# Differential attention: scaling and difference of the two softmax maps made in the turn, by two accumulated products with diagonal matrices

## The chip, the cores and the metric

The kernel is one program on one core of a Trainium2 chip. The metric is device time in microseconds (us) of a whole execution. Three runs of the kernel before took 2820.64, 2817.66 and 2817.2 us, median 2817.66.

Engines are named as in the profile: PE is TensorE's matmul, PEld its weight load, DVE is VectorE, ACT ScalarE, POOL GpSimd and SP SyncE, which issues most DMAs.

## What is computed

The reference is one layer of a hybrid decoder for a prompt of 1024 tokens and eight sample sequences of one new token each, with 2048 tokens in a paged cache. Everything is float32. The part that the change touches is the attention of the prompt:

```
def diff_attn_core(q, k, v, q_pos, k_pos, lam):
    s = einsum("bqhd,bkhd->bhqk", q, k) * (DA_QK ** -0.5)
    s = where(k_pos[None, :] <= q_pos[:, None], s, -inf)
    p = softmax(s, axis=-1).reshape(b, DA_HEADS, 2, tq, tk)
    w = p[:, :, 0] - lam * p[:, :, 1]
    return einsum("bhqk,bkhd->bqhd", w, v)
```

There are 4 heads, each with two maps of 64 columns for query and key and one value of 128 columns. The two feed-forward blocks, the projections and a recurrent branch (RWKV-7) in chunks of 128 tokens stand before and after it in the same program.

## The kernel before

All engines run one program each, whose order is written out by hand; they meet at semaphores. The stages follow each other: feed-forward 1, the projection of query, key and value, the projection for the recurrent branch and the gates, the attention, the recurrent branch in eight chunks, the merge, the output projection, feed-forward 2. The dense stages split each float32 operand in a high and a low part and make three products of each tile (L1792).

The attention has 32 steps, one for each block of 128 queries and each head: `qi = step // 4` is the block of queries, `h = step % 4` the head. A step looks at `n = (qi + 1) * 128` keys, so its width grows from one block of 128 keys to eight, and the 32 steps have 4 * (1 + ... + 8) = 144 blocks. The tile `probs` (`pr` in the code) has two slots, `s = step % 2`, of two maps each. In one step:

- PE makes the scores of a later step in PSUM (L2021), two steps ahead while `qi < 4` and one step ahead after that.
- DVE adds the causal mask to the last block (L1493), takes the maximum of each row (L1495) and scales it (L1496), for each map.
- ACT takes the exponential of each map from PSUM to `probs`, with the row's sum as a by-product (L1062). These are probabilities without their division by the sum.
- DVE takes the reciprocals of the two sums (L1512), multiplies the second by lambda (L1513), scales the second map by it (L1515), and then makes `p1 * inv1 - p2` over the first map (L1517). It tells PE by `w_ready`.
- PE turns each block of the first map to have keys on the partitions (L2042), into PSUM banks 4 and 5. It tells ACT by `w_trans_lo` for the first four blocks and `w_trans_hi` for the others.
- ACT copies the turned blocks to `w_trans` (`wT`, L1086) and tells PE by `w_moved`.
- PE sums the squares of the step before (L2027) and multiplies the values with `w_trans`, block by block (L2056). ACT copies the result (L1095) and squares it (L1100).

Woven in is the attention of the samples. Their softmax is made on DVE in three pieces behind steps 0 to 2 (L1454 to L1474). Their values are 32 groups of four pages, one megabyte a group, which SP loads to a ring of two slots (L560, `value_ring`) and PE weights (L1998) at the places that `FILL_STEP` names: one group in most steps from step 4 on, two in steps 17, 19, 22, 25, 26 and 28. A group is loaded once the second group before it has been used. The four pages are four DMAs.

The tile `tmp` (`T`) has two rows of 1032 columns. Before the attention it holds the gates, whose DMAs to memory (`gate_saved0`, `gate_saved1`, L691) must have landed before it is written again. After the attention it is cut up for the recurrent branch. DVE's first instruction there clears the state (L1532); PE's first is L2079.

These are the lines that weave PE's step together, with much left out:

```
scores(step + 1)                       # one ahead from step 15 on
pe.wait_ge(*ev.at("w_ready", step + 1))
pe.wait_ge(*ev.at("w_moved", step))
for t in range(qi + 1): last = nc.tensor.transpose(...)
pe.wait_ge(*ev.at("w_moved", step + 1))
```

Of the kernel before, what the change touches and what calls it, by code (L numbers as in the profile page):

```python
# [15 lines left out]
P = 128  # L16
# [14 lines left out]
GT = 2 * KT  # L31
# [165 lines left out]
def build(nc, A):  # L197

    ctx = ExitStack()
    with ctx:  # L200
        ev = Events(nc, ctx)
# [6 lines left out]
        def at(name, cols, offset=None, dt=F32):  # L208
            if offset is None:
                offset = place[0]  # L210
                place[0] = (place[0] + cols * 4 + 31) // 32 * 32
            return nc.alloc_sbuf_tensor_at(name, [P, cols], dt, offset=offset)
# [15 lines left out]
        T = at("tmp", 2 * NT)[:, :].rearrange("p (s n) -> p s n", n=NT)  # L228
# [61 lines left out]
        pr = tiles("probs", 8, 4)[:, :, 0:NP].rearrange("p (s m) n -> p s m n", m=2)  # L290
        osq = cols("o_squares", 35, 1024)[:, 512:512 + P]
        osq_sample = cols("o_squares_sample", 35, 1024)[:, 512 + P:512 + P + HP * NS].rearrange("p (h b) -> p h b", h=HP)
        vring = at("value_ring", 8 * 512, base)[:, :].rearrange("p (g j n) -> p g j n", g=2, j=4)
        wT = [at(f"w_trans{s}", NP, base + (4 + s) * KT * P * 4)[:, :] for s in range(2)]
        Wp = cols("s_weights", 35, 512)
        sm = rstd[:, 0:512]
# [189 lines left out]
        STEPS = 8 * HP  # L486
# [21 lines left out]
        FIRST = 4 * HP  # L508
# [690 lines left out]
        def _(dve):  # L1199
# [3 lines left out]
            def in_turn(instruction):  # L1203


                dve.drain()
# [300 lines left out]
            for step in range(STEPS):  # L1507
                qi, s = step // HP, step % 2
                n = (qi + 1) * P
                dve.wait_ge(*ev.at("probs_made", 2 * step + 2))  # L1510
                inv = small[:, 28 + 2 * s:30 + 2 * s]
                in_turn(v.reciprocal(inv, small[:, 18 + 4 * s:20 + 4 * s]))  # L1512
                in_turn(v.tensor_tensor(inv[:, 1:2], inv[:, 1:2], small[:, 3:4], ALU.mult))  # L1513
                p2 = pr[:, s, 1, 0:n]
                in_turn(v.tensor_scalar(p2, p2, inv[:, 1:2], None, ALU.mult))  # L1515
                p1 = pr[:, s, 0, 0:n]
                in_turn(v.scalar_tensor_tensor(p1, p1, inv[:, 0:1], p2, ALU.mult, ALU.subtract).then_inc(ev["w_ready"], 1))  # L1517
                if step + 2 < FIRST:
                    maxima(step + 2)
                if FIRST <= step + 1 < STEPS:  # L1520
                    maxima(step + 1)
                if step < 3:
                    sample_softmax(step)
                for b in range(NS):
                    if FILL_STEP[4 * b + 3] == step - 1:
                        sample_out(b)
                if qi and step % HP == 1:
                    o_inverse(qi - 1)

            dve.wait_ge(*ev.at("gate_saved0", 8 * GT))  # L1530
            dve.wait_ge(*ev.at("gate_saved1", 8 * GT))
            in_turn(v.memset(Ss[0], 0.0).then_inc(ev["ck_s"], 1))  # L1532
            dve.wait_ge(*ev.at("ck_span", 1))
            dve.wait_ge(*ev.at("masks_loaded", 16))

# [236 lines left out]
        def _(pe):  # L1772
# [258 lines left out]
            for step in range(8 * HP):  # L2031
                qi, h, s = step // HP, step % HP, step % 2
                if step + 2 < FIRST:
                    scores(step + 2)
                if FIRST <= step + 1 < 8 * HP:
                    scores(step + 1)
                if step == 2:
                    sample_sums()
                pe.wait_ge(*ev.at("w_ready", step + 1))
                pe.wait_ge(*ev.at("w_moved", step))  # L2040
                for t in range(qi + 1):
                    last = nc.tensor.transpose(PS[:, 4 + t // 4, (t % 4) * P:(t % 4 + 1) * P],  # L2042
                                               pr[:, s, 0, t * P:(t + 1) * P], K("ident"))
                    if t == min(3, qi):
                        last.then_inc(ev["w_trans_lo"], 1)
                    elif t == qi:
                        last.then_inc(ev["w_trans_hi"], 1)
                for k in range(4 * NS):
                    if FILL_STEP[k] == step < FIRST and k % 4:
                        weight_values(k)  # L2050
                pe.wait_ge(*ev.at("w_moved", step + 1))
                if step:
                    pe.wait_ge(*ev.at("o_moved", step))
                    square_sum(step - 1, 6, P)
                for t in range(qi + 1):
                    last = mm(PS[:, 6, 0:P], Vtok[:, t, h * P:(h + 1) * P], wT[s][:, t * P:(t + 1) * P],  # L2056
                              start=(t == 0), stop=(t == qi))
                last.then_inc(ev["o_done"], 1)
                for b in range(NS):
                    if FILL_STEP[4 * b + 3] == step - 1:  # L2060
                        turn_sums(b)
                for f in range(4 * NS):
                    if FILL_STEP[f] == step and (step >= FIRST or f % 4 == 0):
                        weight_values(f)
# [334 lines left out]
```

## Time and profile before

| | |
|---|---|
| runs, median (lowest to highest) | 2817.66 us (2817.2 to 2820.64) |
| span of the profiled execution, first to last instruction | 2812.0 us |
| median of the runs less that span | 5.7 us |
| busy share of PE, PEld, DVE, ACT, POOL | 96%, 91%, 49%, 23%, 10% |
| the attention, from 1331 us on to 1552 us: PE busy | 163.5 us of 221 |
| the same stretch: DVE busy, ACT busy | 146.0 us, 91.4 us |

The page states the span of the profiled execution and no total of its own; what lies around the span is therefore taken as the 5.7 us of the table. The slices of the page are 70.3 us wide, so the attention is slices 19 to 22.

### The profile page before, as it was taken

The numbers are of one execution on the slowest core, as the hardware profiler recorded it, in microseconds if no ns is written. First come the engines' busy times: TensorE is split into PE (matmuls) and PEld (weight loads), VectorE is DVE, ScalarE is ACT, GpSimd is POOL, SyncE is SP. The second block draws the span as 40 slices with busy tenths as digits, with TensorE's granted clock in tenths as the row PEclk, the third lists the DMA queues.
The fourth block names the chain that finished last, engine by engine and source line by source line (L and its number), as shares of the span: only waits on it lengthen the run. The fifth ranks groups of instructions, "written<-read, shape, count | busy, mean of one in ns | idle before, by whom it ended". The sixth has DMA issues, their size and how long they took to land.

```text
span 2812.0 us, 52032 instructions
## 1 busy us (share of the span) xinstructions
PE 2688.0 (96%) x21467; PEld 2549.3 (91%) x21467; DVE 1372.7 (49%) x1461; ACT 659.3 (23%) x1004; POOL 283.2 (10%) x262
## 2 busy tenths in 40 slices
PE   7999999999999999998777999989999999999998
PEld 6999999999999998998344899869999999999998
DVE  4332233223475588777766678675443322322334
ACT  5111111111321222332444223222221111110213
POOL 1000000000011123111100555220000000000000
PEclk8999999999999999999799899989999999999999
DMA  3111111111234435657855100043111111111112
GB/s 106 48 49 45 45 52 45 45 45 43 92 99 123 138 121 192 219 195 255 285 190 177 30 26 26 23 147 130 51 46 52 45 45 45 45 53 45 45 43 77
DMA packets 270207, 252.12 MB, mean 90 GB/s; under 512 B 20725, under 2 KB 216145, under 8 KB 269921
## 3 DMA queue, kind: packets, MB, share of 16 engines
q1 hardware_dynamic: 252960, 189.42, 21.9%
q0 software_dynamic: 16896, 60.40, 5.8%
q8 instruction: 114, 1.87, 0.3%
q14 instruction: 45, 0.36, 0.0%
q10 hardware_dynamic: 192, 0.07, 0.0%
HBM read 209.93 MB, written 39.90 MB: 89 GB/s over the span
## 4 chain that ended last, share of the span: by engine, by line
PE 87%; DVE 7%; SPq 1%; DMA 1%; issue 1%; ACT 1%; DVEq 0%; POOL 0%; ACTq 0%; POOLq 0%
PE ps L1792 74%; PE ps L2097 1%; PE ps L2112 1%; PE ps L1836 1%; PE ps L2117 1%; PE ps L2056 1%; SPq L559 1%; PE ps L1998 1%; SPq L560 1%; DMA q_rot<-q_save 1%; PE ps L2021 1%; PE ps L1955 1%; DMA value_ring<-in_cache_v 1%; PE ps L2144 1%; DVE kq_prod L1362 1%
## 5 line engine op out<-in xcount | busy, mean ns | idle before, releaser
L1792 PE MATMUL ps<-h_hi,w_hi 128*128 128x344 f32 x3072 | 990.0, 322 | 0.0
L1792 PE MATMUL ps<-h_lo,w_hi 128*128 128x344 f32 x3072 | 979.1, 319 | 0.0
L1792 PE MATMUL ps<-h_hi,w_lo 128*128 128x344 f32 x3072 | 978.9, 319 | 0.0
L1792 PEld LDWEIGHTS ps<-h_hi,w_hi 128*128 128x128 f32 x3072 | 576.5, 188 | 15.5 <-issue 14.8
L1792 PEld LDWEIGHTS ps<-h_lo,w_hi 128*128 128x128 f32 x3072 | 576.7, 188 | 2.1 <-issue 1.9
L1792 PEld LDWEIGHTS ps<-h_hi,w_lo 128*128 128x128 f32 x3072 | 576.6, 188 | 0.0
L1792 PE MATMUL ps<-ff_hi,w_hi 128*128 128x344 f32 x1056 | 337.1, 319 | 0.0
L1792 PE MATMUL ps<-ff_lo,w_hi 128*128 128x344 f32 x1056 | 336.6, 319 | 0.0
L1792 PE MATMUL ps<-ff_hi,w_lo 128*128 128x344 f32 x1056 | 336.2, 318 | 0.0
L845 ACT ACTIVATE w_hi<-w_stage 128x1024 fp32r<-128x1024 f32 x194 | 203.9, 1051 | 488.7 <-PE ps L1792 475.2
L1211 DVE TENSOR_TENSOR w_lo<-w_stage,w_hi 128x1024 fp32r<-128x1024 f32 x194 | 238.5, 1229 | 147.7 <-ACT w_hi L845 111.7
L1294 DVE SCALAR_TENSOR_TENSOR x_res<-ps,x_res 128x1032 f32 (+1 forms) x48 | 59.2, 1233 | 297.7 <-PE ps L1792 297.7
L1792 PEld LDWEIGHTS ps<-ff_hi,w_lo 128*128 128x128 f32 x1056 | 198.2, 188 | 0.0
L1792 PEld LDWEIGHTS ps<-ff_lo,w_hi 128*128 128x128 f32 x1056 | 198.2, 188 | 0.0
L1792 PEld LDWEIGHTS ps<-ff_hi,w_hi 128*128 128x128 f32 x1056 | 198.1, 188 | 0.0
L1274 DVE TENSOR_TENSOR tmp<-ps,rstd 128x1032 f32<-128x1032 f32 x44 | 54.2, 1232 | 286.6 <-PE ps L1792 285.0
L1270 DVE TENSOR_TENSOR tmp<-ps,rstd 128x1032 f32<-128x1032 f32 x44 | 54.2, 1233 | 190.9 <-PE ps L1792 190.2
L480 ACT ACTIVATE idle<-idle 128x1 f32<-128x1 f32 x52 | 10.5, 203 | 529.9 <-DVE tmp L1276 457.2
L909 ACT ACTIVATE tmp<-tmp 128x1032 f32<-128x1032 f32 x44 | 46.9, 1067 | 337.9 <-DVE tmp L1270 337.9
L1362 DVE TENSOR_TENSOR kq_prod<-key_ring,rstd 128x2048 f32<-128x2048 f32 x32 | 92.3, 2884 | 3.4 <-issue 1.1
L1278 DVE TENSOR_TENSOR ff_lo<-tmp,ff_hi 128x1032 f32 (+1 forms) x44 | 54.3, 1234 | 70.0 <-ACT ff_hi L914 70.0
L643 POOL DMA_DIRECT2D x_save<-x_res x8 | 4.3, 535 | 774.2 <-DVE x_res L1294 774.2
(410 smaller groups left out, 3235.1 us busy)
## 6 DMA issues: line engine op xcount, KB each, us to landing
w_stage<-in_ffn_up SPq DMA_DIRECT2D x176, 256.0 KB, 3.1
key_ring<-in_cache_k SPq DMA_DIRECT2D x128, 256.0 KB, 2.9
value_ring<-in_cache_v SPq DMA_DIRECT2D x128, 256.0 KB, 2.9
w_stage<-in_w_in SPq DMA_DIRECT2D x84, 256.0 KB, 3.3
w_stage<-in_ffn_down SPq DMA_DIRECT2D x80, 256.0 KB, 3.0
gate_save<-tmp POOLq DMA_DIRECT2D x16, 516.0 KB, 4.5
gate_ring<-gate_save POOLq DMA_DIRECT2D x16, 516.0 KB, 4.6
row_ring<-row_save SPq DMA_DIRECT2D x40, 128.0 KB, 3.0
```

Source lines behind the costliest of these rows:

```text
L559: page = sp.value_load(ptab[0:1, at], min_val=0, max_val=N_PHYS - 1)
L560: sp.dma_start(slot, cache[ds(page, 1)].rearrange("a t n -> (a t) n")).then_inc(ev[done], 16)
L845: sc.activation(whi[s], stg[s], ACT.Copy).then_inc(ev[f"w_high{s}"], 1)
L909: sc.activation(T[:, 0, :], T[:, 0, :], ACT.Silu).then_inc(ev["silu_made"], 1)
L1211: in_turn(v.tensor_tensor(wlo[s], stg[s], whi[s].bitcast(F32), ALU.subtract).then_inc(ev[f"w_split{s}"], 1))
L1270: in_turn(v.tensor_tensor(ch3(T[:, 0, :]), dense[0], ch3(rstd), ALU.mult).then_inc(ev["psum_free0"], 1))
L1274: in_turn(v.tensor_tensor(ch3(T[:, 1, :]), dense[1], ch3(rstd), ALU.mult).then_inc(ev["psum_free1"], 1))
L1278: in_turn(v.tensor_tensor(flat(G[1][:, ds(i, 1), :]), T[:, 1, :], flat(G[0][:, ds(i, 1), :]).bitcast(F32), ALU.subtract).then_inc(ev["ff_l ...
L1294: in_turn(v.scalar_tensor_tensor(ch3(xm), dense[s], 0.5, ch3(xm), ALU.mult, ALU.add)\ .then_inc(ev[f"psum_free{s}"], 1))
L1362: in_turn(v.tensor_tensor(prod.rearrange("p (j n) -> p j n", j=4), kring[:, f % 2], qrow[f // 4 % 2].unsqueeze(1).broadcast_to([P, 4, 512] ...
L1792: last = mm(dense[s][:, j], w[w0][:, k0 + k, :], r[:, k, j * CH:(j + 1) * CH], start=(k == 0 and n == 0), stop=(k == nk - 1 and n == 2))
L1836: last = mm(dense[s][:, j], w[s][:, k, :], r[:, k, j * CH:(j + 1) * CH], start=(k == 0 and n == 0), stop=(k == KT - 1 and n == 2))
```

## The change

The scaling of the two maps and their difference are taken off the whole width of the maps. DVE makes two diagonal matrices of 128 by 128 instead, `inv1 * I` and `-lambda * inv2 * I`, from the identity, in the second row of `tmp` (columns 508 and on, two for each slot). PE multiplies each block of the first map with the first and each block of the second map with the second and sums both in PSUM: one turn of a block becomes two products. The maps stay as ACT wrote them. Since `tmp` is now written in step 0, the wait for the saved gates comes ahead of the first diagonal matrix; and DVE waits, after it has cleared the state, for the last turns, because `tmp` is used anew behind that.

```
+        shares = [[T[:, 1, 508 + (2 * s + m) * P:508 + (2 * s + m + 1) * P] for m in range(2)] for s in range(2)]
...
                 in_turn(v.tensor_tensor(inv[:, 1:2], inv[:, 1:2], small[:, 3:4], ALU.mult))
-                p2 = pr[:, s, 1, 0:n]
-                in_turn(v.tensor_scalar(p2, p2, inv[:, 1:2], None, ALU.mult))
-                p1 = pr[:, s, 0, 0:n]
-                in_turn(v.scalar_tensor_tensor(p1, p1, inv[:, 0:1], p2, ALU.mult, ALU.subtract).then_inc(ev["w_ready"], 1))
+                if step == 0:
+                    dve.wait_ge(*ev.at("gate_saved0", 8 * GT))
+                    dve.wait_ge(*ev.at("gate_saved1", 8 * GT))
+                in_turn(v.tensor_scalar(shares[s][0], K("ident"), inv[:, 0:1], None, ALU.mult))
+                in_turn(v.tensor_scalar(shares[s][1], K("ident"), inv[:, 1:2], -1.0, ALU.mult, ALU.mult)
+                        .then_inc(ev["w_ready"], 1))
...
             in_turn(v.memset(Ss[0], 0.0).then_inc(ev["ck_s"], 1))
+            dve.wait_ge(*ev.at("w_trans_hi", STEPS - FIRST))
...
                 for t in range(qi + 1):
-                    last = nc.tensor.transpose(PS[:, 4 + t // 4, (t % 4) * P:(t % 4 + 1) * P],
-                                               pr[:, s, 0, t * P:(t + 1) * P], K("ident"))
+                    for m in range(2):
+                        last = mm(PS[:, 4 + t // 4, (t % 4) * P:(t % 4 + 1) * P], pr[:, s, m, t * P:(t + 1) * P],
+                                  shares[s][m], start=(t % 4 == 0 and m == 0), stop=(t % 4 == 3 or t == qi) and m == 1)
```

PE's program at steps 28 and 29, the first two of full width, before. L1998 are values of the samples, L2021 scores, L2042 the turns, L2027 the sum of squares, L2056 the values of the prompt; `x8` counts products in the program's terms.

```order
L1998 MATMUL ps<-value_ring,s_weights 4x512 x4
L2021 MATMUL ps<-k_rot,q_rot 128x512 x4
L2042 MATMUL ps<-const,probs 128x128 x8
L2027 MATMUL ps<-o_squares,const 1x128
L2056 MATMUL ps<-w_trans_106,v_tok 128x128 x8
L1998 MATMUL ps<-value_ring,s_weights 4x512 x8
```

The same place of PE's program in the changed kernel, whose lines stand four or five further down:

```order
L2002 MATMUL ps<-value_ring,s_weights 4x512 x4
L2025 MATMUL ps<-k_rot,q_rot 128x512 x4
L2047 MATMUL ps<-tmp,probs 128x128 x16
L2031 MATMUL ps<-o_squares,const 1x128
L2061 MATMUL ps<-w_trans_106,v_tok 128x128 x8
L2002 MATMUL ps<-value_ring,s_weights 4x512 x8
```

Nothing has moved; eight turns with the identity have become sixteen products with `tmp`, where the diagonal matrices lie.

DVE's program at step 0, before, from the maximum of step 1 on, with the semaphores that it waits for:

```order
L1496 TENSOR_SCALAR small<-small 128x2
L1512 RECIPROCAL small<-small 128x2 [waits s_x_moved0]
L1513 TENSOR_TENSOR small<-small 128x1
L1515 TENSOR_SCALAR probs<-probs,small 128x128
L1517 SCALAR_TENSOR_TENSOR probs<-probs,small 128x128
```

The same place in the changed kernel:

```order
L1497 TENSOR_SCALAR small<-small 128x2
L1513 RECIPROCAL small<-small 128x2 [waits s_x_moved0]
L1514 TENSOR_TENSOR small<-small 128x1
L1518 TENSOR_SCALAR tmp<-const,small 128x128 [waits s_params_loaded2,s_x_saved]
L1519 TENSOR_SCALAR tmp<-const,small 128x128
```

The order is the same; the two instructions over the maps have become two of 128 columns in every step, and the first of them waits here for the saved gates, which share the two semaphores named.

## Rows read from the trace of the kernel before

**Rows 1.** The page: granted clock in 40 slices, and the chain by line.

```profile
PEclk8999999999999999999799899989999999999999
...
PE ps L1792 74%; PE ps L2097 1%; PE ps L2112 1%; PE ps L1836 1%; PE ps L2117 1%; PE ps L2056 1%; SPq L559 1%; PE ps L1998 1%; SPq L560 1%; DMA q_rot<-q_save 1%; PE ps L2021 1%; PE ps L1955 1%; DMA value_ring<-in_cache_v 1%; PE ps L2144 1%; DVE kq_prod L1362 1%
```

**Rows 2.** Stretches of the attention: busy us (instructions), clock, DMA share, GB/s.

```profile
1331.00:1552.00 221.00, 163.50 (x1040) 88.69 (x1044) 146.04 (x320) 91.42 (x256) 17.31 (x26) 0.88 0.65 216
...
1331.30:1364.20 32.90, 20.32 (x78) 9.38 (x79) 23.34 (x61) 11.19 (x47) 11.56 (x22) 0.51 0.99 389
...
1504.30:1511.00 6.70, 6.69 (x23) 2.27 (x23) 0.95 (x2) 0.60 (x1) 0.00 (x0) 0.55 0.69 236
```

**Rows 3.** Groups by line, 1331 to 1552: busy, mean ns, idle before.

```profile
L2056 PEld LDWEIGHTS ps<-w_trans,v_tok 128*128 128x128 f32 x288 | 38.2, 208 | 9.1 <-issue 8.4 <-ACT w_trans L1086 0.7
L1517 DVE SCALAR_TENSOR_TENSOR probs<-probs,small 128x128 f32<-128x128 f32 (+7 forms) x32 | 26.9, 842 | 2.4
L2042 PE MATMUL ps<-const,probs 128*128 128x128 f32 x144 | 24.5, 299 | 19.2 <-DVE probs L1517 19.0
L1515 DVE TENSOR_SCALAR probs<-probs,small 128x128 f32<-128x128 f32 (+7 forms) x32 | 16.8, 523 | 2.8 <-issue 0.4
```

**Rows 4.** Waits, 1331 to 1552: total us, times, longest.

```profile
PEld ps L2042 <- DVE probs L1517: 30.7, 22, 5.1
PE ps L2027 <- ACT w_trans L1086: 19.8, 22, 1.2
PEld ps L1998 <- DMA value_ring<-in_cache_v: 16.2, 11, 4.0
PE ps L1998 <- DMA value_ring<-in_cache_v: 11.4, 9, 3.0
```

**Rows 5.** Timeline of one step of full width: start, us, engine, line, [idle before].

```profile
1524.67 1.99 PE L2021 MATMUL ps<-k_rot,q_rot 64*128 64x512 f32 x8
1524.73 1.29 DVE L1517 SCALAR_TENSOR_TENSOR probs<-probs,small 128x1024 f32<-128x1024 f32 x1
...
1526.59 0.85 PEld L2042 LDWEIGHTS ps<-const,probs 128*128 128x128 f32 x8 [0.76 <-DVE probs L1517]
...
1528.86 0.38 PE L2027 MATMUL ps<-o_squares,const 128*1 128x128 f32 x2 [1.17 <-ACT w_trans L1086]
...
1529.17 1.86 PEld L2056 LDWEIGHTS ps<-w_trans,v_tok 128*128 128x128 f32 x16 [0.22 <-issue]
...
1531.15 1.04 PE L1998 MATMUL ps<-value_ring,s_weights 128*4 128x512 f32 x8
```

**Rows 6.** DVE's scaling at 128 columns alone, groups by line and form.

```profile
L1515 DVE TENSOR_SCALAR probs<-probs,small 128x128 f32<-128x128 f32 x4 | 1.3, 315 | 0.7 <-issue 0.4
```

**Rows 7.** Timeline, PE: the two longest waits for DVE, steps 3 and 31.

```profile
1353.64 0.48 PE L2042 MATMUL ps<-const,probs 128*128 128x128 f32 x1 [4.43 <-DVE probs L1517]
...
1543.67 1.25 PE L2042 MATMUL ps<-const,probs 128*128 128x128 f32 x8 [3.69 <-DVE probs L1517]
```

**Rows 8.** Timeline, PE: the longest wait for values, and work at the lower clock.

```profile
1504.31 1.89 PE L1998 MATMUL ps<-value_ring,s_weights 128*4 128x512 f32 x8 [3.03 <-DMA value_ring<-in_cache_v]
1506.13 3.79 PE L2021 MATMUL ps<-k_rot,q_rot 64*128 64x512 f32 x8
...
1546.61 3.78 PE L2056 MATMUL ps<-w_trans,v_tok 128*128 128x128 f32 x16
...
1555.90 1.97 PE L2097 MATMUL ps<-chunk_work 64*64 64x64 f32 x32 [2.24 <-DVE chunk_work L1548]
...
1576.88 1.15 PE L2097 MATMUL ps<-chunk_work 64*64 64x64 f32 x32
```

**Rows 9.** The last DMA of the gates, and DVE's first scaling.

```profile
1325.93 0.53 POOL L691 DMA_DIRECT2D gate_save<-tmp  x1 [10.74 <-ACT tmp L1030]
...
gate_save<-tmp POOLq DMA_DIRECT2D x1, 516.0 KB, 6.9
...
1335.38 0.40 DVE L1515 TENSOR_SCALAR probs<-probs,small 128x128 f32<-128x128 f32 x1
```

## The prediction

> **What bounds the kernel now.** I read the page first: 74% of the chain that ended last is one line of the dense stages, which the change leaves alone, and the granted clock has its lowest slices, a 7 and an 8, in and next to the attention [rows 1]. So I cut that stretch out: in the 221 us from 1331 to 1552, PE is busy 163.5, DVE 146.0, ACT 91.4 [rows 2]. No engine is full; they hand work to each other. Then I asked for the groups and the waits of this stretch alone. The reader is to see that PE carries most of the work and that its idle time of 57.5 us has three large causes: DVE's scaled maps (19.0 us before the turns by the PE row, 30.7 by the row of its weight loads), ACT's copy of the turned blocks (19.8 us in 22 waits), and the samples' values (11.4 us on PE, 16.2 on PEld) [rows 3, 4]. The PE row counts the tail of a product as busy and so understates a wait; the PEld row overstates it, since the tail still runs. Each wait is bounded by the two.
>
> Last I read a step of full width in the timeline [rows 5]: scores from 1524.67, turns from 1526.59, squares from 1528.86, values from 1529.17, the samples' group from 1531.15. All that PE waits in it is 0.76 us before the turns by the PEld row and 1.17 before the squares. PE is close to being the bound of a wide step already, and the change gives work to PE.
>
> **Removed from DVE.** The two instructions over the maps go: 16.8 + 26.9 = 43.7 us [rows 3]. Two of 128 columns come in each of 32 steps, at the 0.315 us that the same form takes at that width [rows 6]: 64 x 0.315 = 20.2. DVE is freed of some 23 us, but only where PE waits for it does this shorten anything.
>
> **Added to PE.** A turn of a block is one instruction, 144 in all; a product in float32 is two, as the 288 of the values' line for the same 144 blocks show [rows 3]. In the step of rows 5 eight turns load in 0.85 us, 0.107 each, and the values' sixteen instructions in 1.86 us, 0.116 each. With two products a block costs 4 x 0.116 = 0.466 us where it cost 0.107: 0.359 more, 51.7 for 144 blocks. It grows with the width: 1.4 us in the four steps of one block, 11.5 in the four of eight. The product with a diagonal matrix is not in the trace. From below, one could cost as little as a turn, 0.107; then 15.4 us are added in all. From above, I take the mean of the values' loads over the whole stretch, slow clock included, 38.2 / 288 = 0.133 [rows 3], which would make it 61. I take 0.116, the row nearest in kind: same shapes, same step.
>
> From 1331.3 to 1364.2 the granted clock is 0.51 [rows 2], the 1.2 GHz level, and the first ten blocks run in it (four steps of one block, three of two), so they cost twice: 3.6 us more if the clock comes back where it does now, 1.4 if it is back by step 4. I take 2.5. Added: 54.2 us.
>
> **What falls away.** (a) Waits of the turns for DVE. In the step of rows 5 DVE's second instruction began at 1524.73 and ended at 1526.02. The second diagonal matrix, 0.3 us long, would be ready by about 1525.1 at the latest, before the scores end; so the wait goes there, and in all wide steps. The waits of the first four steps stay, since DVE makes the samples' softmax in them: 8.6 us by the PE row, the last and largest 4.43. Of the 3.69 in the last step some 1.3 stay, since the reciprocals start late there [rows 7]. By the PE row this leaves 19.0 - 8.6 - 1.3 = 9.1 to gain; by the PEld row 30.7 less about 13, 18. I take 12.
>
> (b) Waits for the samples' values. SP needs a fixed time after a group has been used to have the next but one there, and every step that becomes longer by 0.7 (two blocks) to 2.9 us (eight) meets its values later. The largest such wait, 3.03 [rows 8], stands in a step of seven blocks, whose turns grow by 2.5. Of the 11.4 to 16.2 us [rows 4] some 2 stay: 9 to 14 to gain. I take 10.
>
> (c) ACT's copy. It must follow the turns, and the 1.17 of rows 5 stays. But in narrow steps ACT is still at exponentials when the turns end, and longer turns cover that. Of 19.8 us in 22 waits [rows 4], 0 to 6; I take 4.
>
> (d) The lower clock. Behind the wait of 3.03 us the granted clock was 0.55 [rows 2]; the samples' group took 1.89 us and the scores 3.79, against 1.04 and 1.99 at full clock; behind the wait of 3.69 the values took 3.78 against about 2.05 (their loads 1.86) [rows 5, 7, 8]. These make 4.4 us. Two shorter falls in the slices between I put at 2.6: 7 in all, if PE, nearly always at work, keeps 2.4 GHz; bounds 0 and 8. The recurrent branch begins at the lower clock too: 1.97 us for a group of products that takes 1.15 later [rows 8]; over some four groups 3 us, bounds 0 and 4.
>
> **Edits that I cost at nothing.** DVE's wait for the gates in step 0: the last of their DMAs goes out at 1325.93 and lands 6.9 us later, about 1333, and DVE reaches the place at 1335.38 [rows 9]. The cover is 2.5 us; were the DMA later by more, each us would be paid in full, since the maximum of step 2 and the samples' softmax are queued behind it and PE waits for both. DVE's wait after clearing the state: behind it stand three small preparations, about 3 us, and then work on products that PE gives only after copy, squares and values of the last step, about 4 us; that hides them. No instruction of POOL or SP moves.
>
> **The sum.** 51.7 + 2.5 - 12 - 10 - 4 - 7 - 3 = +18.2 us on a span of 2812.0. With the terms at their ends it is +3 (51.7 + 1.4 - 18 - 14 - 6 - 8 - 4) or +46 (61 + 3.6 - 9.1 - 9). The 5.7 us around the span stay, so the median of 2817.7 becomes 2835.9; I say 2836.
>
> A check on two steps, from the turns at 1526.59 to those of the last step at 1543.67 [rows 5, 7]: 17.1 us. After, the first has turns 16 x 0.233 = 3.73, then 1.42 until the squares as now (2.27 - 0.85), 2.29 for squares and values, 0.97 for the samples and 1.93 for scores: 10.3. The second has 3.73 + 1.42 + 2.29, a small product of 0.95, and the 1.3 that stays: 9.7. That is 20.0, so +2.9 of 5.7 added; the one long wait does it. In the same 10.3 DVE and ACT need some 9, so they are not late instead of PE. For all steps the sum keeps 18 of 54.
>
> **Rivals.**
>
> *The clock does not come back* (2847). For it: a wait of 1.2 us in each step stays. Against it: the falls of now stand behind waits above 3 us. Then (d) is nought, and some of the added turns run at half: 18.2 + 10 + 1 = +29.
>
> *The clock comes back sooner* (2831). The stretch at 0.51 holds 20.3 us of PE work [rows 2]; if it ends four to eight steps in, 3 to 5 us of that come back, all of 1.4 to 2.5 in the added turns with it: 18.2 - 5 = +13. For it: PE has more to do in each step. Against it: the first four steps wait for DVE as before. The Trainium skill, in TensorE: Matmul & The Clock Gate, Part 4, says that a transposition doesn't count as work for the clock as a product does; by that this case would be the likelier one. No row here tells the two apart.
>
> *Not slower: PE's idle time takes it all* (2813). Place: the turns. Price: a product at the pace of a turn, 0.107. Then 15.4 + 0.5 is added, and 12 for DVE, 4 for values and ACT, and 5 of the clock fall away: -5. It decides from an added 0.15 us a block down, which is 21 us over 144. For it: the mean PE times of the two lines are close in the timeline, since a tail is in both. Against it: 144 against 288 instructions [rows 3], which the engine runs one after the other.
>
> *Mostly absorbed* (2824). The waits are worth their PEld values, 18 + 14 + 6 in place of 26: +6. For it: the PE row does hide waits. Against it: the check on two steps, the most favourable pair, keeps half of what is added.
>
> **Chances.** My forecast, +10 to +26: 0.62. Clock sooner, within that range: 0.10. Clock stays low: 0.12. Absorbed: 0.11. Not slower: 0.05. The range for 8 times in 10 takes the first three and half of the absorbed case: 2822 to 2850. A measurement of this kernel tells 0.2%, 5.6 us, from no change: faster is below 2812, slower above 2823.3. Faster 0.04 (most of the not-slower case lies at its edge), within 0.10, slower 0.86.
>
> **What would show it.** In the changed profile: the turns' line with 576 matmul instructions and loads of 3.7 us in a step of full width (half of that would be the rival of the cheap product); DVE's scaling as 64 instructions of about 0.3 us; PE's wait for DVE at 12 us or less by the PE row, with only the first four steps large; its wait for values down to some 2 us; a granted clock of full level from about 1375 on into the recurrent branch. The forecast is wrong if waits for ACT grow, because the copy of the turned blocks comes later and the exponentials queue behind it; or if DVE waits at its first diagonal matrix.

## The result, and the profile after

The changed kernel took 2836.05 us, the median of 4 runs (2835.06 to 2840.39), against 2817.43 of 4 runs of the kernel before on the same chip (2812.34 to 2820.64): a ratio of 1.0069, 95% interval 1.0054 to 1.0083. It is slower by 19 us, where 18.2 were forecast. In a second comparison the same pair gave 1.0077 (1.0057 to 1.0096), so the change costs 15 to 27 us, and what follows takes 19 to 22. One of the 29 executions of the kernel before beside the last four kernels took 3001.0 us at a granted clock of 0.837, and every figure here leaves it out.

The page of the changed kernel's profile, whose execution took 2836.46 us with a span of 2834.3; engines first, then the granted clock in 40 slices of 70.9 us.

```profile
PE 2729.3 (96%) x21899; PEld 2599.6 (92%) x21899; DVE 1346.6 (48%) x1461; ACT 659.0 (23%) x1004; POOL 282.3 (10%) x262
...
PEclk9999999999999999998999999989999999999999
```

PE has 432 instructions more (before: 21467) and is busy 41 us longer; DVE is busy 26 us less (1372.7 before). The 7 and 8 in and next to the attention have become a single 8 [rows 1].

Stretches of the attention in the changed kernel, columns as in [rows 2].

```profile
1331.00:1552.00 221.00, 190.38 (x1343) 126.38 (x1344) 112.42 (x300) 81.64 (x223) 10.70 (x21) 0.95 0.62 196
1331.30:1364.20 32.90, 23.91 (x108) 14.32 (x108) 23.52 (x64) 11.35 (x46) 10.41 (x20) 0.64 0.98 377
1364.00:1500.00 136.00, 121.41 (x901) 81.52 (x902) 66.09 (x181) 53.90 (x143) 0.00 (x0) 1.00 0.60 178
...
1560.30:1567.10 6.80, 6.29 (x31) 6.29 (x32) 0.72 (x2) 0.00 (x0) 2.73 (x3) 0.53 0.30 34
```

In the same 221 us PE is busy 190.4, where it was 163.5 [rows 2], and it is not done: the first product of the recurrent branch stands at 1571.7 (L2084), 245.4 us after the first scores at 1326.3. Before, that stretch was 1331.5 to 1551.1, 219.6 us. PE is the busiest engine by far; DVE fell from 146.0 to 112.4. From first scores to first product PE is busy 205.7 of the 245.4 us, before 162.6 of 219.6: 43.1 us more of work and 17.3 less of idle time. From 1364 to 1500 the clock is at its full level, 2.4 GHz, throughout. (The windows stand at the same times as in [rows 2], though the attention begins 5.2 us earlier in this trace; what that means for the 219.6 and the 245.4 is taken up under *again*.)

Groups by line of the changed kernel, 1331 to 1573, as in [rows 3]; its L2047 was L2042, L2061 was L2056, L1518 and L1519 stand for L1515 and L1517.

```profile
L2047 PE MATMUL ps<-tmp,probs 128*128 128x128 f32 x576 | 78.6, 294 | 10.3 <-DVE tmp L1519 10.3
L2047 PEld LDWEIGHTS ps<-tmp,probs 128*128 128x128 f32 x576 | 71.9, 204 | 25.3 <-DVE tmp L1519 13.3 <-issue 11.4
L2061 PEld LDWEIGHTS ps<-w_trans,v_tok 128*128 128x128 f32 x288 | 35.4, 194 | 8.2 <-issue 7.6 <-ACT w_trans L1087 0.7
L1518 DVE TENSOR_SCALAR tmp<-const,small 128x128 f32<-128x128 f32 x32 | 10.1, 316 | 2.9 <-issue 0.4
L1519 DVE TENSOR_SCALAR tmp<-const,small 128x128 f32<-128x128 f32 x32 | 10.0, 313 | 2.5
```

There are 576 product instructions, four a block, and DVE's two lines take 20.1 us where they took 43.7.

Waits of the changed kernel, 1331 to 1575, as in [rows 4]; L2031 was L2027, L2002 was L1998.

```profile
PE ps L2031 <- ACT w_trans L1087: 19.1, 22, 1.2
PEld ps L2047 <- DVE tmp L1519: 13.3, 7, 4.3
PE ps L2047 <- DVE tmp L1519: 10.3, 6, 3.6
...
PEld ps L2002 <- DMA value_ring<-in_cache_v: 7.3, 7, 2.7
PE ps L2002 <- DMA value_ring<-in_cache_v: 4.4, 4, 1.8
```

The wait for DVE went from 19.0 to 10.3 us by the PE row and the one for the values from 11.4 to 4.4; ACT's hardly moved (19.8 before).

A step of full width in the changed kernel's timeline, to set beside [rows 5].

```profile
1539.15 3.65 PEld L2047 LDWEIGHTS ps<-tmp,probs 128*128 128x128 f32 x32 [0.76 <-issue]
...
1544.16 0.38 PE L2031 MATMUL ps<-o_squares,const 128*1 128x128 f32 x2 [1.17 <-ACT w_trans L1087]
...
1544.47 1.86 PEld L2061 LDWEIGHTS ps<-w_trans,v_tok 128*128 128x128 f32 x16 [0.22 <-issue]
...
1546.82 0.29 DVE L1518 TENSOR_SCALAR tmp<-const,small 128x128 f32<-128x128 f32 x1
1547.18 0.29 DVE L1519 TENSOR_SCALAR tmp<-const,small 128x128 f32<-128x128 f32 x1
1547.43 1.99 PE L2025 MATMUL ps<-k_rot,q_rot 64*128 64x512 f32 x8
1549.35 3.65 PEld L2047 LDWEIGHTS ps<-tmp,probs 128*128 128x128 f32 x32 [0.76 <-issue]
```

The products load in 3.65 us, where eight turns took 0.85. The diagonal matrices are ready at 1547.47, almost 2 us before PE wants them, so DVE is off the path. By these rows PE waits in 10.2 us for its own issue (0.76) and for ACT (1.17).

The last step and the start of the recurrent branch in the changed kernel's timeline, to set beside [rows 7, 8].

```profile
1558.05 0.16 DVE L1514 TENSOR_TENSOR small<-small 128x1 f32<-128x1 f32 x1
1558.27 1.18 POOL L736 TENSOR_TENSOR chunk_work<-kk,tmp 128x512 f32<-128x512 f32 x1 [216.56 <-ACT tmp L1075]
1558.28 1.25 DVE L1518 TENSOR_SCALAR tmp<-const,small 128x128 f32<-128x128 f32 x1
1559.41 1.26 POOL L737 TENSOR_TENSOR chunk_work<-b_vec,tmp 128x512 f32<-128x512 f32 x1
1559.61 1.15 DVE L1519 TENSOR_SCALAR tmp<-const,small 128x128 f32<-128x128 f32 x1
...
1560.81 6.44 PEld L2047 LDWEIGHTS ps<-tmp,probs 128*128 128x128 f32 x32 [3.38 <-DVE tmp L1519]
...
1567.56 0.27 DVE L1639 MEMSET tmp<- 128x256 f32 x1 [6.29 <-PE ps L2047]
...
1572.94 0.69 DVE L1550 TENSOR_TENSOR chunk_work<-ps,loop_masks 128x512 f32<-128x512 f32 x1 [4.60 <-PE ps L2088]
...
1575.66 1.15 PE L2102 MATMUL ps<-chunk_work 64*64 64x64 f32 x32 [2.44 <-DVE chunk_work L1552]
```

Here a diagonal matrix takes 1.25 and 1.15 us instead of 0.29, beside two instructions of POOL, PE's loads wait 3.38, and at 0.53 of the clock the last products load in 6.44 us. DVE's new wait after clearing the state ends at 1567.56, and DVE still waits 4.60 for PE later: that edit costs nothing, as forecast. So does the one for the gates:

```profile
1330.76 0.29 DVE L1518 TENSOR_SCALAR tmp<-const,small 128x128 f32<-128x128 f32 x1
```

### The profile page after: what moved, and what is told of

Same layout as the page of the kernel before. It is cut to its first block, busy times and chain, and to the rows that moved or that the text cites. A ratio compares the mean times of both kernels' runs of the same rounds, so it can differ in the third digit from the quotient of the medians.

```text
span 2834.3 us, 52897 instructions
## 1 busy us (share of the span) xinstructions
PE 2729.3 (96%) x21899; PEld 2599.6 (92%) x21899; DVE 1346.6 (48%) x1461; ACT 659.0 (23%) x1004; POOL 282.3 (10%) x262
## 4 chain that ended last, share of the span: by engine, by line
PE 90%; DVE 5%; ACT 1%; issue 1%; SPq 1%; DMA 1%; POOL 0%; DVEq 0%; ACTq 0%; POOLq 0%
PE ps L1796 74%; PE ps L2047 2%; PE ps L2102 1%; PE ps L2061 1%; PE ps L2025 1%; PE ps L2117 1%; PE ps L2122 1%; PE ps L2002 1%; PE ps L1840 1%; PE ps L1959 1%; PE ps L2157 1%; PE ps L2149 1%; ACT w_trans L1087 1%; PE ps L2129 0%; SPq L560 0%
## 5 line engine op out<-in xcount | busy, mean ns | idle before, releaser
L1796 PEld LDWEIGHTS ps<-h_hi,w_hi 128*128 128x128 f32 x3072 | 576.5, 188 | 15.5 <-issue 14.8
L1275 DVE TENSOR_TENSOR tmp<-ps,rstd 128x1032 f32<-128x1032 f32 x44 | 54.2, 1232 | 286.5 <-PE ps L1796 284.9
L2047 PEld LDWEIGHTS ps<-tmp,probs 128*128 128x128 f32 x576 | 71.9, 204 | 25.3 <-DVE tmp L1519 13.3
L2047 PE MATMUL ps<-tmp,probs 128*128 128x128 f32 x576 | 78.6, 294 | 10.3 <-DVE tmp L1519 10.3
```

Of the source, the lines that this page charges most:

```text
L1275: in_turn(v.tensor_tensor(ch3(T[:, 1, :]), dense[1], ch3(rstd), ALU.mult).then_inc(ev["psum_free1"], 1))
L1796: last = mm(dense[s][:, j], w[w0][:, k0 + k, :], r[:, k, j * CH:(j + 1) * CH], start=(k == 0 and n == 0), stop=(k == nk - 1 and n == 2))
L2047: last = mm(PS[:, 4 + t // 4, (t % 4) * P:(t % 4 + 1) * P], pr[:, s, m, t * P:(t + 1) * P], shares[s][m], start=(t % 4 == 0 and m == 0), s ...
```

## The experiments

Each execution lists its span and its mean granted clock. From them comes a number that the text uses throughout, the time at the 1.2 GHz level in a whole execution: (1 - clock) * 2 * span, here "low-clock time", as the mean of the executions of a kernel with its standard error. The clock is listed to three decimals, so that one execution has it to some 3 us. The times of the kernel before are those of its executions on the same chip beside the others: median 2818.09 of 15 with low-clock time 134.4 +- 2.5 us (first four kernels), 2819.71 of 25 with 133.2 +- 2.7 (next four), 2820.1 of 28 with 135.3 +- 1.9 (last four).

**again**: the changed kernel once more, without an edit.

> The changed kernel once more, as the base of the others on the same chip. Theory (turns' added work is on the path, waits give back part): +18 to +22 us over the kernel before. It also tells how far profiles of one kernel differ before the attention begins, where nothing is changed: the first scores began at 1326.3 us in the changed kernel's trace and 1331.5 before.

2839.99 us of 4 runs, ratio 1.0077 (1.0057 to 1.0096), low-clock time 112.1 +- 2.7. The stretch from first scores to the first product of the recurrent branch was 246.9 us. The result stands; what is new is that the low-clock time is 22 us shorter than before. (The four executions of the first comparison give 103.5 +- 4.3.)

The traces also differ where nothing is changed. The first scores stand between 1325.1 and 1331.5 us in the 14 traces, latest in that of the kernel before, whose attention is the shortest, 219.6 us; its execution is one of the quick ones, too. The trace of before_pool_later (below), the same kernel up to the last step, has 1328.7 and 227.7 us. So the length of a stretch in a single trace is uncertain by some 8 us, and the 25.8 us between 219.6 and 245.4 are not the price of the change; that is taken from the medians of executions.

**narrow_only** and **wide_only**: the change in steps 0 to 15 alone (40 of the 144 blocks), and in steps 16 to 31 alone (104). PE's loop is divided in the same way as DVE's part, which is shown.

```
+                if step < FIRST:       # wide_only: step >= FIRST; FIRST is 16
                     in_turn(v.tensor_scalar(shares[s][0], ...
+                else:
+                    in_turn(v.tensor_scalar(p2, p2, inv[:, 1:2], ...
```

> The change in steps 0 to 15 alone (one to four blocks); steps 16 to 31 are those of the kernel before. Theory A (narrow steps are bound by DVE and by the samples' values, so PE's added work is hidden there): 14.4 us are added at full clock and nearly all is hidden, 0 to +4 us over the kernel before. Theory B (each block added costs the same share of itself, 18.6 of 51.7): 14.4 x 0.36 = +5. Theory C (all of it is paid): +14.

> The change in steps 16 to 31 alone (five to eight blocks). 37.3 us are added to PE. Theory A (wide steps are bound by PE): +17 to +21 over the kernel before, the whole of the change's cost. Theory B (even share): 37.3 x 0.36 = +13.

Narrow alone: 2822.47 us of 9 runs, ratio 1.0015 (1.0000 to 1.0030), low-clock time 125.3 +- 2.8. Wide alone: 2836.79 of 4, 1.0068 (1.0048 to 1.0089), 116.2 +- 4.9. Of 14.0 us of work added in the narrow steps (40 blocks by 0.349) 4 are left, of 36.3 in the wide steps 19. The wide steps carry the change, and the two parts make up the whole: 4.2 + 19.2 = 23.4 against 21.7 by the ratios, within the intervals.

**relief_only**: DVE makes the two diagonal matrices, but PE turns the first map by transposes as before. Scaling and difference are left out.

```
                 for t in range(qi + 1):
-                    for m in range(2):
-                        last = mm(..., pr[:, s, m, t * P:(t + 1) * P], shares[s][m], ...)
+                    last = nc.tensor.transpose(..., pr[:, s, 0, t * P:(t + 1) * P], K("ident"))
```

> DVE makes the two diagonal matrices as in the changed kernel, but PE turns only the first map, with the transposes of the kernel before: scaling and difference are left out. This is DVE's relief without PE's added work. Theory (the wait for DVE is worth between its PE row and its PEld row, 9 to 18 us, but values and copy then come forward as the next wait): -5 to -12 us against the kernel before. Rival (DVE was off the path; the relief is worth nothing): 0 to -2.

2809.38 us of 7 runs, ratio 0.9967 (0.9956 to 0.9979): the relief of DVE alone is worth 9 us. Its waits, as in [rows 4]:

```profile
PEld ps L2002 <- DMA value_ring<-in_cache_v: 19.7, 12, 4.7
PEld ps L2046 <- DVE tmp L1519: 18.5, 11, 5.1
PE ps L2002 <- DMA value_ring<-in_cache_v: 14.3, 10, 3.7
PE ps L2046 <- DVE tmp L1519: 13.6, 8, 4.4
```

PE's wait for DVE fell by 5.4 us by its own row and by 12.2 by the loads' row, and the wait for the samples' values grew by 3 by both: when steps become shorter, the values are late instead. So the two waits must not be added as if each stood by itself. The changed kernel loses on top of this gain what its products cost.

**ident_product**: the kernel before, with its turns as ordinary products with the identity, so two instructions a block where there was one, and nothing else.

```
-                    last = nc.tensor.transpose(PS[...], pr[:, s, 0, t * P:(t + 1) * P], K("ident"))
+                    last = mm(PS[...], pr[:, s, 0, t * P:(t + 1) * P], K("ident"), start=(t % 4 == 0), stop=...)
```

> The kernel before with one thing changed: each turn is an ordinary product with the identity, not a transpose. DVE works over the whole maps as before. A float32 product is two instructions, so PE gets 144 x (0.228 - 0.107) = 17.4 us more, 12.6 of it in wide steps. Theory (price of the product is two instructions of 0.114; without DVE's relief the waits for DVE stay, only values and clock give back): +8 to +14 us over the kernel before. Rival (a product with a diagonal matrix goes at a turn's pace): 0.

2818.94 us of 10 runs, ratio 1.0002 (0.9991 to 1.0013), low-clock time 112.7 +- 3.8. The expectation failed: 17.4 us of added work (144 by 2 * 0.114 - 0.107) cost nothing. The work is there:

```profile
L2042 PEld LDWEIGHTS ps<-const,probs 128*128 128x128 f32 x288 | 37.2, 203 | 34.5 <-DVE probs L1517 28.8 <-issue 5.3
...
PE ps L2042 <- DVE probs L1517: 17.4, 10, 4.7
...
PE ps L1998 <- DMA value_ring<-in_cache_v: 7.0, 5, 3.5
```

The loads take 37.2 us where they took 16.0. Waits gave back 6.5 by the PE rows (1.6 DVE, 4.4 values, 0.5 ACT), and the low-clock time is 20.5 us shorter, which at half the pace is worth 10.3.

**one_map**: the changed kernel with the product of the first map alone. The second map is left out.

```
-                    for m in range(2):
-                        last = mm(..., pr[:, s, m, ...], shares[s][m], ...)
+                    last = mm(..., pr[:, s, 0, ...], shares[s][0], ...)
```

> The changed kernel with the first map's product alone; the second map is left out of the result. PE loses 144 x 0.228 = 32.8 us against the changed kernel, DVE keeps its relief. Theory (the relief alone was worth 9 us; on top of it 17.4 us of PE work, which now is mostly on the path in wide steps): 0 to +6 us over the kernel before, 15 to 20 below the changed kernel. Rival (even share of 36%): the kernel before minus 9 plus 6, -3.

2817.52 us of 10 runs, ratio 0.9992 (0.9983 to 1.0002), low-clock time 114.9 +- 3.6. That is a little quicker than the 0 to +6 us expected. Against relief_only the first product in place of a turn costs 7 us of its 17.4, by the ratios; the changed kernel, with the second product as well, costs 22 to 24 us more than this one, of 32.8 (144 by 0.228).

**third_product**: the changed kernel with the first map's product made once more, so that the first map counts twice.

```
-                    for m in range(2):
+                    for m in range(3):          # m % 2 picks the map and its matrix
```

> The changed kernel with a third product in each block, the first map's once more; the result has the first map twice. 144 x 0.228 = 32.8 us are added to PE, 23.7 in wide steps and 9.1 in narrow ones. Theory (after the change PE is the bound of every wide step and nearly of the narrow ones): +26 to +33 us over the changed kernel, a slope of 0.8 to 1. Rival (waits go on giving back two thirds): +12.

2866.46 us of 4 runs, ratio 1.0167 (1.0145 to 1.0189), low-clock time 111.7 +- 6.8. Another 32.8 us of work cost about 26 (by the ratios to before, 1.0167 - 1.0077 = 0.0090, or 25; by the first comparison's 1.0069, 28), at the lower end of what was expected, and far from the rival's 12. Its rows:

```profile
PE ps L2047 <- DVE tmp L1519: 8.6, 4, 3.3
...
PE ps L2002 <- DMA value_ring<-in_cache_v: 1.4, 2, 0.7
```

Of the waits that gave back before hardly any are left (ACT's, 19.1 us, stays in every version), and the low-clock time no longer falls.

**one_pass**: the changed kernel with maps and diagonal matrices in float32r, in which a product is one instruction.

```
+        prr = tiles("probs_r", 8, 4, F32R)...      # the same memory as probs
-                        last = mm(..., pr[:, s, m, ...], shares[s][m], ...)
+                        last = mm(..., prr[:, s, m, ...], sharesr[s][m], ...)
```

> The changed kernel with maps and diagonal matrices in the reduced float32r format, so that each product should be one instruction; the result loses precision. Theory (what costs is the number of instructions, 0.114 us each, not that they are products): 288 in place of 576 in this line, the time of the one-map kernel, 0 to +6 us over the kernel before. Rival (the format changes the pace of an instruction too): by the loads of the line in a step of full width, 1.83 us if the pace is the same, other if not.

2827.03 us of 10 runs, ratio 1.0026 (1.0013 to 1.0039), low-clock time 138.4 +- 2.7. A step of full width in its timeline:

```profile
1532.54 1.86 PEld L2051 LDWEIGHTS ps<-tmp_r,probs_r 128*128 128x128 f32 x16 [0.76 <-issue]
```

The same place in one_map:

```profile
1526.54 1.86 PEld L2046 LDWEIGHTS ps<-tmp,probs 128*128 128x128 f32 x16 [0.76 <-issue]
```

Same count, same pace, and two products for the price of one. By the ratios it is 12 to 14 us better than the changed kernel and still 7 us behind the kernel before, just outside the 0 to +6 expected. It is also 9.5 us behind one_map, whose count and pace of instructions it shares; half the difference in low-clock time (138.4 against 114.9) is 11.8 us, enough for all of it.

**turned_twice** and **relief_twice**: the kernel before, and relief_only, with each transpose made twice. In relief_twice scaling and difference are left out.

```
+                    for _ in range(2):
                         last = nc.tensor.transpose(...)
```

> The kernel before with each turn made twice by the transpose, into the same place: 288 turn instructions, as many as the kernel whose turns are products with the identity has. That one cost nothing, and its runs had 113 us of half clock in the mean (from the mean granted clock and span of 10 runs) against 133 for the kernel before. Theory (a product counts as work for the clock and a transpose does not, so the product pays for itself with clock): 144 x 0.107 = 15.4 us are added, half clock stays near 133 us or above, +6 to +12 us over the kernel before. Rival (any instruction counts alike, and the added work fell into waits): half clock near 113 us and a time within 3 us of the kernel before.

> The kernel with DVE's relief alone, with each turn made twice by the transpose; scaling and difference are left out, as in that kernel. To be read beside the one-map kernel, whose turns are one product each at nearly the same instruction pace: -0.8 per mille to the kernel before, 115 us of half clock in the mean of 10 runs. Theory (transposes don't count for the clock): half clock 125 to 140 us and 4 to 8 us above the one-map kernel, so +2 to +6 over the kernel before. Rival (they count alike): half clock near 115, time of the one-map kernel or 1 us less.

turned_twice: 2819.44 us of 12 runs, ratio 0.9998 (0.9987 to 1.0009), low-clock time 116.5 +- 3.9. relief_twice: 2815.94 of 12, 0.9989 (0.9978 to 0.9999), 122.9 +- 2.7. A step of full width of turned_twice:

```profile
1529.76 1.73 PEld L2043 LDWEIGHTS ps<-const,probs 128*128 128x128 f32 x16 [0.76 <-issue]
```

Sixteen transposes take 1.73 us, 0.108 each, so some 15.4 us are added over 144 blocks, and they cost nothing, just as 17.4 us of products did. The low-clock time falls by 19 us with them and by 20.5 with the products. So added transposes shorten it as well as products do; that a product takes the place of a transpose isn't what does it. relief_twice is less clear. Its time is that of one_map, as the rival had it, but its low-clock time, 122.9 +- 2.7, lies between the two values that were expected and is no lower than that of relief_only (124.3 +- 5.4): the second transposes shortened nothing there that the runs can tell.

**before_pool_later** and **after_pool_later**: the kernel before and the changed kernel, with POOL's first work for the recurrent branch held until DVE has finished the last step's part.

```
             pool.wait_ge(*ev.at("value_used", 4 * NS))
+            pool.wait_ge(*ev.at("w_ready", STEPS))
             gram_sides(0)
```

> The kernel before with one wait more: POOL begins the recurrent branch's products (L735 on) only when DVE has scaled the maps of step 31. In the trace DVE's last instruction over the maps took 2.04 us beside POOL's, against 1.28 in the step before. Theory (the two share a path to memory, and DVE's end is on the path there): the last one takes 1.3 us, PE's wait before the last turns 3.7 becomes about 3; -0.5 to -1 us, within what can be told. Rival (POOL's products come late now and the first blocks of the recurrent branch wait for them): +1 to +3.

> The changed kernel with the same wait of POOL. There DVE's two diagonal matrices of the last step took 1.25 and 1.15 us beside POOL's products against 0.29 each in the steps before, PE waited 3.3 us for them, and the last turns ran at half clock, 6.4 us of loads against 3.65. Theory: the matrices take 0.3 each again, the wait becomes about 1.5, and with a shorter wait the clock may stay, 2.8 more: -1.8 to -4.6 us against the changed kernel, whose median was 2836 and 2840. Rival (the wait is DVE's reciprocal behind the samples' last product, not POOL): no change.

before_pool_later: 2816.96 us of 12 runs, ratio 0.9996 (0.9983 to 1.0009). after_pool_later: 2834.6 of 6, 1.0060 (1.0042 to 1.0077). Last step of the first, then of the second:

```profile
1547.72 1.28 DVE L1518 SCALAR_TENSOR_TENSOR probs<-probs,small 128x1024 f32<-128x1024 f32 x1
1549.06 0.86 PEld L2043 LDWEIGHTS ps<-const,probs 128*128 128x128 f32 x8 [3.02 <-DVE probs L1518]
```

```profile
1558.35 0.29 DVE L1519 TENSOR_SCALAR tmp<-const,small 128x128 f32<-128x128 f32 x1
1558.71 0.29 DVE L1520 TENSOR_SCALAR tmp<-const,small 128x128 f32<-128x128 f32 x1
1559.05 5.28 PEld L2048 LDWEIGHTS ps<-tmp,probs 128*128 128x128 f32 x32 [1.56 <-DVE tmp L1520]
```

With POOL out of the way the difference over 1024 columns takes 1.28 us instead of 2.04, and PE's loads wait 3.02 instead of 3.78; the diagonal matrices take 0.29 us again, and the loads wait 1.56 instead of 3.38. That is 2 us in the changed kernel, in whose time it doesn't show beyond the intervals. No version beats the kernel before with the whole computation in it.

**One account for all.** The work added to PE at full clock, the change in its three waits by the PE rows (for DVE, the values and ACT, from one profile each, against [rows 4]) and half the change in low-clock time give:

| kernel | work | waits | clock | sum | measured (ratio * 2818, 95%) |
|---|---|---|---|---|---|
| again | +50.3 | -17.1 | -11.2 | +22.0 | +21.7 (16 to 27) |
| narrow_only | +14.0 | -7.3 | -4.6 | +2.1 | +4.2 (0 to 8) |
| wide_only | +36.3 | -8.7 | -9.1 | +18.5 | +19.2 (14 to 25) |
| relief_only | 0 | -2.1 | -5.1 | -7.2 | -9.3 (-12 to -6) |
| ident_product | +17.4 | -6.5 | -10.3 | +0.6 | +0.6 (-3 to 4) |
| one_map | +17.4 | -9.7 | -9.2 | -1.5 | -2.3 (-5 to 1) |
| third_product | +83.1 | -21.1 | -10.8 | +51.2 | +47.1 (41 to 53) |
| one_pass | +18.1 | -6.9 | +2.6 | +13.8 | +7.3 (4 to 11) |
| turned_twice | +15.4 | -5.0 | -9.4 | +1.0 | -0.6 (-4 to 3) |
| relief_twice | +15.4 | -8.5 | -6.2 | +0.7 | -3.1 (-6 to 0) |
| before_pool_later | 0 | +0.5 | -3.4 | -2.9 | -1.1 (-5 to 3) |
| after_pool_later | +50.3 | -18.4 | -14.8 | +17.1 | +16.9 (12 to 22) |

Ten of twelve sums lie within their intervals; one_pass and relief_twice come out lower than their sums by 6.5 and 3.8 us. The account is no sharper than its terms: the intervals are 5 to 12 us wide, the clock column has standard errors of 2 to 4 us, and the waits come from one trace each. The waits of before_pool_later, 50.7 us in sum against 50.2 in [rows 4], show that at least the base of that column repeats. Half the low-clock time is an upper bound of what it costs, since waits in it cost the same at either level.

## Why the prediction was right

The forecast was right in sign, in size (18.2 against 18.6 in the first comparison and 21.9 in the second) and in the mechanism. By its steps:

- **Added to PE.** Forecast 51.7 at full clock; measured at 0.114 an instruction (3.65 / 32) it is 50.3. The loads' group grew from 16 to 71.9 us, all clocks included, 55.9 for 54.2 forecast. The 0.116 of the row nearest in kind was the right choice; a product with a diagonal matrix costs what any does, and the rival of the cheap product falls.
- **DVE's freed time.** Forecast 43.7 to 20.2, measured 20.1.
- **(a) Waits for DVE.** Forecast -12, within 9.1 and 18; measured -8.7 by the PE row and -17.4 by the loads' row. The account above closes with the PE row, so the term was too large by 3: by its own PE row the forecast was 9.1, and the step to 12 was what failed. That 9.1 was nearly met is partly luck, since two errors cancel in it. The first four steps kept 6.2 us instead of 8.6, and the last kept 3.3 us instead of 1.3: the forecast put the diagonal matrices at 0.315 us everywhere, and beside POOL they took 1.25 and 1.15. after_pool_later gives the forecast's number, 1.5.
- **(b) Waits for values.** Forecast -10, with 2 us left; measured -7.0, with 4.4 left (-7.9 in the repeat). relief_only shows why it is no term of its own: shorter waits for DVE bring the values' wait back.
- **(c) ACT's copy.** Forecast -4, measured -0.7. This step failed. Longer turns were to cover the time in which ACT is still at exponentials; but ACT's copy follows the last turn in either kernel, and PE waits in the same 22 places as before. The lower bound, 0, was right.
- **(d) and the chunk's start: the clock.** Forecast -7 and -3, less 2.5 for added turns at the low level. The falls near 1385, 1409 and 1504 are gone, full clock holds from 1355.5 on to 1560.3, short of the recurrent branch into which it was to hold, and a first group of the recurrent branch runs in 1.15 us; but new falls stand at 1560.3 to 1567.1 and 1577.4 to 1584.2. In total low-clock time fell by 22 us in the repeat, worth 11 and not 7.5. From the first product of the recurrent branch on, the changed kernel is not quicker: 1262.6 us against 1260.9, so the term of 3 us was not there, and more than it came back within the attention.
- **The sum.** The waits were taken at 26 us and gave 17; the clock was taken at 7.5 net and gave 11; the work was 1.4 less: 18.2 + 9 - 3.7 - 1.4 = 22. Two errors of opposite sign, a few microseconds each, made the median look better hit than the steps were.
- **The check on two steps.** Forecast 10.3 and 9.7 us, measured 10.2 (1539.15 to 1549.35; 11.05 for a step with two groups of values, 1528.10 to 1539.15) and 11.46 (1549.35 to 1560.81), the second longer by the wait beside POOL. From the first turn to the last step's it is 21.7 us, where 20.0 were forecast and 17.1 measured before: +4.6 and not +2.9.
- **Around the span.** Forecast 5.7 us, measured 2.2 (2836.46 - 2834.3), and 1.7 to 2.2 in every run. The 5.7 compared the span of one execution with the median of others: with 2.2 around its span the profiled one was 3.5 us quicker than the median. The sum was a difference and isn't touched by it.

Of the rivals, *the clock does not come back* is refuted: from 1364 to 1500 the clock is 1.00. *The clock comes back sooner* was half right: the first stretch at the low level ended 29.2 us after the first scores (at 1355.5) instead of 32.7, and low-clock time fell by more than forecast. But the reason given beside it doesn't hold. The Trainium skill, in TensorE: Matmul & The Clock Gate, Part 4, has it that a transposition doesn't count as work for the clock; in turned_twice doubled float32 transposes shortened the low-clock time from 135.3 +- 1.9 to 116.5 +- 3.9 us, as much as products with the identity did (133.2 +- 2.7 to 112.7 +- 3.8). Here the measurement decides. It doesn't show that transposes count for as much as products: relief_twice leaves that open. *Mostly absorbed* takes every wait at the loads' row and is 13 to 16 us off. Yet absorption is real for the first 17 us: in ident_product and turned_twice all of what was added is absorbed, by the account about a third by waits and the rest by the clock. *Not slower* named 21 us of added work as the point from which the time rises. That is near what the runs gave: with DVE's relief, 17.4 us of added work (one_map) gave -2.3 us and 50.3 gave 19 to 22, so a straight line between them crosses zero near 21. The rival failed on its price: the added work was 50.3 us and not 15.4. The 33 us beyond the changed kernel's cost about 26.

What stays open: why float32r products leave the low-clock time at 138.4 us, where float32 products of the same count and pace bring it to 114.9. one_map reads one map of each block in two instructions, one_pass reads both in one each, so the format isn't the only difference, and no run parts the two. The waits of one_pass for DVE and values are 2.7 us longer by the PE rows; nor is it shown whether that is cause or effect.

## What to carry to other kernels

Moving work from an engine that is half idle to one that is three quarters busy pays only up to the waits of the receiver: price it in instructions (a float32 product is two), and compare it with what the receiver waits for by its own row, not by that of its loads. Waits of one chain aren't independent: when one goes, the next supplier (here the samples' values) is late instead, so take the best single relief as an experiment by itself (relief_only, -9 us) and not as a sum. Small additions to a PE that idles in gaps can be free: of ident_product's 17.4 us the waits gave back 6.5 and the shorter low-clock time 10.3. That this happened for 15 us says nothing for the next 30.

## What the runs showed of the hardware

- **PE's added work can shorten the time at the low clock, once.** Before, 133 to 135 us of an execution are at the 1.2 GHz level. In ident_product, turned_twice, wide_only and one_map, 15 to 36 us of added work in the attention, transposes or float32 products, went with 113 to 117 us; 83 us of it bring it no lower (111.7 +- 6.8). What that is worth, some 10 us, was not expected for additions as small. It is no rule: 18 us of float32r products left it at 138.4 +- 2.7, and relief_twice's transposes at 122.9 +- 2.7, where DVE's relief alone had 124.3 +- 5.4.
- **A float32 transpose of 128 by 128 is one instruction and takes 0.107 us back to back** (16 in 1.73 us), a float32 product two of 0.114, a float32r product one of 0.116 (16 in 1.86 us).
- **DVE and POOL delay each other.** DVE's scaling of 128 columns took 0.29 us alone and 1.25 beside an instruction of POOL that began 0.01 us earlier and took 1.18; the next took 1.15 beside the next of POOL. In the kernel before, the difference over 1024 columns took 2.04 us in the last step and 1.28 with POOL held back; the POOL instruction that began during it took 2.25 us where its like takes 1.26. The Trainium skill, in SBUF — State Buffer, section "SBUF: two separate sides", says that DVE, for certain forms of its instructions, and GpSimd share a pair of ports as an exclusive lock, held for the whole instruction, by which the loser is fully blocked. The trace agrees: DVE's instructions end 0.08 and 0.09 us after POOL's (1559.53 against 1559.45, 1560.76 against 1560.67).
- **Executions of one kernel differ by 12.5 us** (2812.3 to 2824.9, 25 of the kernel before on one chip), more than half of what the whole change costs.
